# ScalarE takes the newest exponential ahead of the copies of turned tiles, in both attention loops of a two-layer encoder

## The reference

```python
def block(i):                                   # fox: 128 queries against all earlier keys
    s = jnp.einsum('bqhd,bkhd->bhqk', qb, k).astype(jnp.float32) * scale
    s = s + cq[..., :, None] - cum[..., None, :]
    s = jnp.where(key_pos[None, :] <= qpos[:, None], s, NEG_INF)
    p = jax.nn.softmax(s, axis=-1).astype(v.dtype)
    return jnp.einsum('bhqk,bkhd->bqhd', p, v)

def chunk(c):                                   # band: 64 queries against 9 chunks of keys
    s = jnp.einsum('bqhd,bkhd->bhqk', qs, ks).astype(jnp.float32) * scale + bias
    s = jnp.where((key_pos >= 0)[None, :], s, NEG_INF)
    p = jax.nn.softmax(s, axis=-1).astype(vs.dtype)
    return jnp.einsum('bhqk,bkhd->bqhd', p, vs)
```

## Time and profile before

| | us |
|---|---|
| median of 3 runs | 3267.31 |
| lowest and highest | 3263.86, 3271.94 |
| the profiled execution | 3267.52 |
| its span, first to last instruction | 3265.8 |
| first to last row maximum and residue, fox | 267.9 |
| the same, band | 238.8 |

### The profile page before, as it was taken

The page is one execution under the profiler, slowest core; times in us unless marked ns, Lnnn a source line. Parts: engine busy times, 40 slices in busy tenths (PEclk is TensorE's granted clock), DMA queues, the critical chain, the costliest instruction groups (busy, mean ns, idle before and its releaser), DMA issues. The chain is left out here.

```text
span 3265.8 us, 42768 instructions
## 1 busy us (share of the span) xinstructions
PE 3091.4 (95%) x15696; PEld 2595.0 (79%) x15696; DVE 1343.7 (41%) x2522; ACT 1008.3 (31%) x2234; POOL 427.0 (13%) x769
## 2 busy tenths in 40 slices
PE   8999689979999999999989997997999999999998
PEld 6877489867788888888878886887778888888887
DVE  3122178863433333333333221886633333333333
ACT  4232067731321111111133222776132111112112
POOL 0000088850000000000000001342300000000000
PEclk9999799989999999999999998999999999999999
DMA  4888187753411111111016985876321111111101
GB/s 152 200 228 233 60 274 252 249 129 115 167 39 54 49 44 46 39 39 39 0 65 180 250 206 187 274 257 182 104 84 39 39 39 39 39 39 39 48 30 58
DMA packets 357852, 375.89 MB, mean 115 GB/s; under 512 B 28720, under 2 KB 297024, under 8 KB 353488
## 3 DMA queue, kind: packets, MB, share of 16 engines
q1 hardware_dynamic: 357712, 374.07, 37.4%
HBM read 257.33 MB, written 130.42 MB: 119 GB/s over the span
## 5 line engine op out<-in xcount | busy, mean ns | idle before, releaser
L291 PE MATMUL ffn_gu<-ffn_gh,ffn_xh 128*128 128x512 f32 x1584 | 639.5, 404 | 0.0
L292 PE MATMUL ffn_gu<-ffn_gl,ffn_xh 128*128 128x512 f32 x1584 | 623.1, 393 | 0.0
L293 PE MATMUL ffn_gu<-ffn_gh,ffn_xl 128*128 128x512 f32 x1584 | 617.0, 390 | 0.0
L1547 DVE TENSOR_TENSOR all_h<-ffn_dn,all_h 128x1024 f32<-128x1024 f32 x198 | 242.5, 1225 | 353.8 <-PE ffn_dn L293 353.8
L1531 DVE TENSOR_TENSOR ffn_hid<-ffn_gu,ffn_gate 128x256 f32<-128x256 f32 x198 | 84.0, 424 | 726.6 <-ACT ffn_gate L1524 726.6
L293 PEld LDWEIGHTS ffn_gu<-ffn_gh,ffn_xl 128*128 128x128 f32 x1584 | 298.8, 189 | 67.0
L291 PEld LDWEIGHTS ffn_gu<-ffn_gh,ffn_xh 128*128 128x128 f32 x1584 | 298.0, 188 | 60.0
L292 PEld LDWEIGHTS ffn_gu<-ffn_gl,ffn_xh 128*128 128x128 f32 x1584 | 298.8, 189 | 55.0
L1524 ACT ACTIVATE ffn_gate<-ffn_gu 128x256 f32<-128x256 f32 x198 | 75.7, 382 | 837.5 <-PE ffn_gu L293 837.5
L291 PE MATMUL ffn_dn<-ffn_dh,ffn_hidh 128*128 128x512 f32 x792 | 308.4, 389 | 2.9 <-DVE ffn_hidl L1542 2.9
L293 PE MATMUL ffn_dn<-ffn_dh,ffn_hidl 128*128 128x512 f32 x792 | 308.7, 390 | 0.0
(11 more groups left out here) (241 smaller groups left out, 5346.5 us busy)
## 6 DMA issues: line engine op xcount, KB each, us to landing
ffn_graw<-in_w_gate_up SPq DMA_DIRECT2D x40, 1024.0 KB, 7.5
ffn_draw<-in_w_down SPq DMA_DIRECT2D x22, 1024.0 KB, 4.9
fox_ks<-k_split SPq DMA_DIRECT2D x16, 1088.0 KB, 5.0
band_ks<-k_split SPq DMA_DIRECT2D x16, 1088.0 KB, 5.1
qkvw_raw<-in_w_a_in SPq DMA_DIRECT2D x5, 2048.0 KB, 9.7
out<-qkvw_stage SPq DMA_DIRECT2D x36, 256.0 KB, 2.7
q_high<-qkvw_th SPq DMA_DIRECT2D x72, 128.0 KB, 2.4
q_low<-qkvw_tl SPq DMA_DIRECT2D x72, 128.0 KB, 2.4
```

The lines of the kernel that those rows point to most:

```text
L291: pe.matmul(out, xh, wh, start=first, stop=False)
L292: pe.matmul(out, xh, wl, start=False, stop=False)
L293: return pe.matmul(out, xl, wh, start=False, stop=last)
L1547: dve.tensor_tensor(h[:, t, :], dn[:].rearrange("p a n -> p (a n)"), h[:, t, :], ALU.add).then_inc(dn_used, 1)
```

## The change

In ACT's list of a step the exponential of unit s-1 changes places with the high copies of unit s-3. The loop is shared, so both attentions change. Lists of the other engines, semaphores and their counts, buffers and instructions stay as they are.

```diff
                 for s in STEPS:
                     n = turned_at(s)
+                    if 0 <= s - 1 < N:
+                        exp(s - 1)
                     if n is not None:
                         high(n)
-                    if 0 <= s - 1 < N:
-                        exp(s - 1)
                     if begun_at(s) is not None:
                         begun(begun_at(s))
```

## The result

| | us |
|---|---|
| before, median | 3267.03 |
| changed kernel, median of 4 runs | 3540.11 (3537.59 to 3541.18) |
| the profiled execution of it | 3537.59, span 3535.9 |

The ratio is 1.0833, with a 95% interval of 1.0815 to 1.0852: 273 us slower. The forecast was 3505 us with a range of 3455 to 3590.

What follows compares the result with a forecast made beforehand. PE was taken to bound the loops before, and a ring of DVE and ACT operations after: 390.0 + 354.2 = 744.2 us against 506.7, so 3267.5 + 237.5 = 3505 us, range 3455 to 3590.

Steps and rivals of the forecast that it cites:

- The bound: Both attention loops before: PE sets the pace, busy 253.5 of 267.9 us in fox and 225.0 of 238.8 in band.
- The wait that moves: ACT's queue, both loops: the wait for the maximum of s-1 now stands ahead of the high copies of s-3.
- The sum of the ring: Both loops: maxima, exponentials, first high copies and residues add to 390.0 us in fox, 354.2 in band, against 506.7 together before.
- the ring: DVE and ACT, each step: maximum, exponential, first high copy, residue, next maximum, one after another; 2.71 us fox, 2.46 band.
- PE's cover: PE in both loops: its 1.76 and 1.56 us a step fit beside 2.71 and 2.46, costed at nothing extra.
- the likeliest path: Both loops run at the ring's length with PE at full clock: 237.5 us added, 3505 us; chance 0.74.
- The sign given for it: PE in both loops: its busy share falls to about 65%.
- case (b): Both loops: gaps make PE's clock fall; about 3563 us, up to 3622 at the lower level throughout; chance 0.18.
- the ring's bounds: Whole kernel, ring alone: links 17 us fewer or 23 more, durations 22 either way; about 3470 to 3540 us.
- Case (a): Both loops: earlier exponentials help PE; 3260.6 us, or 3239 if all PE's idle time there went; chance 0.04.
- Case (c): Both loops: nothing happens, engines work past a waiting instruction or ACT's 25% idle takes the wait; 3267 us; chance 0.04.
- Outside the loops: All other stages: no instruction is touched, costed at nothing, they keep their length.

Runs made afterwards that it cites:

- the filled kernel: Changed kernel plus 21 matmuls without use per head, from the second head on, in PE's gaps ahead of the streams' begin: 3506.58 us, ratio to before 1.0734.
- the older exponential: Changed kernel, but ACT takes the exponential of unit s-2 instead of s-1 ahead of the high copies: 3265.49 us, ratio to before 0.9999.

## Why the prediction was right, and by how much it was off

**The bound.** Right: in the kernel before, work added to PE costs time (50 us for 630 matmuls), and an instruction added to ACT costs a sixth of its time.

**The wait that moves.** Right, and it carries the result. The chain maximum, exponential, copy, residue, maximum stands in the trace step by step, and the two idle times grew as its order says. Ahead of fox's exponentials 188.6 us of waiting lie in the loop, against 191 forecast (the group's 201.8 holds 13.1 us from before the loop, and the 28.6 that the forecast compares with holds as much); ahead of the residues it is 155.6 us (136.9, and 18.7 for the stream units) against 164.

**The sum of the ring.** Right in size. 390.0 and 354.2 us were worked out; with PE kept at work the loops took 392.1 and 354.3. The durations and links read from single rows held, since the means of the groups did not move.

**PE's cover.** This step failed: I cost PE at nothing on the likeliest path, at the full clock. Its steps do fit at the upper level, as the filled kernel shows. But the clock did not stay there, and at the lower level the step with sixteen value matmuls ahead of the transposes came late, by 2.1 us in every second head of fox and 0.2 to 1.4 us in most heads of band. That is 32.6 us of waits, most of the distance from 3505 to 3540. The sign given for it failed too: PE is busy 79% and 78% of the loops, not 65%, since its work takes longer at the lower clock.

**The rivals.** By the forecast's own sign, loops longer than the ring with the clock well below 0.9, what came is the ring with the clock's case (b) on top, and not the likeliest path. I gave (b) 0.18 and took half of its full price, 58 us. It came about in both loops at 0.81 and 0.84 and cost 35 us, since a slowed PE still hides beside the ring for most of a head. The rule from the Trainium skill that was set beside it, TensorE: Matmul & The Clock Gate, section "A second HAM failure mode: psum-queue depth-cycling", was borne out: with short idle times between groups of matmuls, 1.51 us at most in the stretch shown, the clock went from 1.00 to 0.50 and back to 1.00 within 16 us. The time alone would not have told (b) from the likeliest path: the ring's bounds, simply added up, reach 3550 and not 3540; the clock, the waits and the filled kernel tell it. Case (a), a gain, had 6.9 us of waits to offer. PE's waits for exponentials are gone from the changed loops, but the ring costs forty times as much; the gain by itself was not measured. Case (c) is refuted by the result, and by the 0.155 us that an ACT instruction costs in the ring, though ACT idles half of the time.

**Outside the loops.** Nothing there, as forecast: the rest of the span differs by 2.7 us.

## What to carry to other kernels

Before an instruction is moved ahead of others in an in-order queue, write down what it waits for and follow the queues from there: if the path leads back through another engine to the same instruction one step later, the sum of that ring is the least that a step can take, however idle the engines are. Write the queue out over two steps, too: the lists by step can look changed while the order is the same, as with the older exponential, and it is the order over two steps that decides whether the ring closes in one step or in two. Where a ring leaves PE with gaps, count its work at the lower clock too, in the longest step, not on average.

## What the runs showed of the hardware

The granted clock fell although PE had not stood idle for long: in the stretch shown PE was busy 1.46, 1.26 and 0.69 us of three times two, with no wait over 1.51 us, and the clock was at 0.50 in the 2 us after. In the kernel before the falls that I had looked at followed a stretch of 2 us without any PE work. And work without use made a kernel faster: 630 matmuls more, 33.5 us less.
